# PEER gate spreading beside the u matmuls: second keys compared four tokens at once, routing weights applied on ScalarE

## The chip, the cores and the metric

The kernel runs on one core of one Trainium2 chip. The metric is the device time of one launch in microseconds. Names of engines in the trace: PE is TensorE (PEld its weight loads), DVE is VectorE, ACT is ScalarE, POOL is GpSimd, SP issues the DMAs.

## What is computed

Two trunk layers run over 288 tokens (256 prompt, 32 sample). Each layer has a token mixer and then a PEER block with 128 x 128 single-neuron experts. Only the PEER block matters here:

```python
def one_block(xb):
    q = (xb @ wq).reshape(blk, PEER_HEADS, 2, KEY_DIM)
    s = jnp.einsum('thcd,hcnd->thcn', q.astype(jnp.float32), keys.astype(jnp.float32))
    sv, si = lax.top_k(s, PEER_TOPK)
    ...
    expert = i1 * N_KEYS + i2
    gate = jax.nn.softmax(best, axis=-1)
    h = jnp.einsum('thkd,td->thk', u_tab[expert], xb)
    coef = (gate * jax.nn.gelu(h.astype(jnp.float32))).astype(xb.dtype)
    return jnp.einsum('thk,thkd->td', coef, v_tab[expert])
```

8 heads choose 16 experts each, so a token has 128 chosen experts, each with a first key, a second key and a softmax weight.

## The kernel before

**The PEER block computes every expert densely.** 128 weight tiles of `u` (32 groups `U` of RING = 4 tiles) each give one 128 x 288 block of `gelu(h)` in `acts`; it is multiplied by a dense gate matrix, which is zero but for the chosen experts, and then by 128 tiles of `v`. fp32 weights are split into a high and a low part and a product takes three matmuls (L608 to L610). For each half of a weight tile ScalarE copies the high part (`w_high`), GpSimd subtracts the low part (`w_low`), and the matmuls of a later tile use both. ScalarE makes the high part two tiles ahead, into the buffer that the half just multiplied leaves free, so its copy waits for that half's products.

**The gate matrix** is made for four tokens at a time, a batch: 72 batches a layer. For each token `one1` (128 slots x 128, one where the column is the slot's first key) and `one2` (the weight of the slot where the column is its second key) are multiplied on TensorE (`gates_of`, L779) into a PSUM bank, `bank[4]` for even batches and `bank[5]` for odd ones. `routed` transposed to `selT` holds first key, second key and weight of slot (partition) and token (column). `hot_iota` and `hot_tiles` are copies of the comparison rows in PSUM.

**The spreading stage** is where the change lies. It stands once in each layer beside 12 tiles of `u` (DURING), six batches a tile, three after each half. TensorE's order in a tile is: products of half a, batches 0, 1, 2, products of half b, batches 3, 4, 5. Even and odd here are also even and odd batches, since a tile begins at a multiple of six.

- VectorE: `onehots_of(k)` makes `one2` with four instructions of 128 columns (comparison and weight in one, L1478) and for even batches `one1` in one instruction of 512 (L1474). `weigh(k)` (L1485) multiplies the rows already in `acts` by the gate bank. It runs `weigh(k)` as soon as batch k is spread, and then `onehots_of(k + 2)`.
- ScalarE: in each half it first copies the high part (L1042), which waits for the products of that half; in half b the gelu of the tile follows (L1045). Then come three `keep_spread(k)` (L1032), which copies the rest of the gate bank once `weigh(k)` is done, and so lets TensorE overwrite the bank with batch k + 2.
- GpSimd: in a tile it subtracts the low part of half a (L589), makes `one1` of the odd batch 3 (`odd_onehot`, four instructions, L576), subtracts half b, makes `one1` of batch 5 and of batch 1 of the next tile. The `one1` of an odd batch waits for the odd batch before it.
- TensorE: batch k waits for `onehots`, for `odd_onehots` if odd, and for `spread_kept` of batch k - 2.

All engines run their own program in order; only semaphores tie them.

Of the kernel before, what the change touches and what calls it, by code (L numbers as in the profile page):

```python
# [33 lines left out]
ALU = mybir.AluOpType  # L34
ACT = mybir.ActivationFunctionType
AX = mybir.AxisListType

P = 128
# [62 lines left out]
def group(name, g):  # L101

    return g + FIRST[name]


def number(name, g, s):

    return RING * group(name, g) + s
# [7 lines left out]
BATCHES = T // 4  # L116
GGROUPS = 3
UREST = UGATED + GGROUPS
BEFORE, DURING = RING * UGATED, RING * GGROUPS
AFTER = BEFORE + DURING  # L120
TILE_BATCHES = BATCHES // DURING
HALF_BATCHES = TILE_BATCHES // 2

# [39 lines left out]
def build(nc, w_first, x_in, params_in, final_in, pool_first, ext_in, h0_in, w_in, w_pool, w_lru, w_ab, w_c, w_d, w_out,  # L163
          w_q, w_keys, w_u, w_v, x_keep, y_out, ext_out, h_out):
    with ExitStack() as ctx:
        def sem(name):
            return ctx.enter_context(nc.semaphore(name))
# [42 lines left out]
        selT = keep("selT", [3, T])  # L210
        o_one = cursor[0]
        one1 = [keep(f"one1_{b}", [4, P]) for b in range(2)]
        one2 = [keep(f"one2_{b}", [4, P]) for b in range(2)]
# [17 lines left out]
        def over(name, slot, c, dt=F32, skip=0):  # L231
# [77 lines left out]
            sem(n) for n in ("turned", "turned_out", "onehots", "spread", "spread_out"))  # L309
        odd_onehots, spread_kept, during_gated, tile_gated = (  # L310
            sem(n) for n in ("odd_onehots", "spread_kept", "during_gated", "tile_gated"))
        next_high, next_low = sem("next_high"), sem("next_low")
        stored, v_step, route_step = sem("stored"), sem("v_step"), sem("route_step")
        first_sem, last_sem = landed[0], route_step
# [139 lines left out]
        with nc.Fori(0, DEPTH) as layer:  # L454
            with nc.Block() as block:
# [146 lines left out]
                def _(pe):  # L602
# [60 lines left out]
                    for s, src in enumerate(("p_b", "xconv", "xconv", "xconv")):  # L663
                        pe.wait_ge(pooled if s == 0 else c_conv, 1)
                        high, low = pair[src]
                        for k0, wh, wl, count in halves("S", 0, s):
                            k0 += 4 * (s == 3)
                            for k in range(4):
                                if n >= 4:
                                    pe.wait_ge(extra_out, n - 3)  # L670
                                last = product(res[4 + n % 4], wh[:, k, :], wl[:, k, :],
                                               (high[:, k0 + k, :], low[:, k0 + k, :]), True, True)
# [29 lines left out]
                    for s in range(RING):  # L702
                        if s == LN_TILES[0]:
                            pe.wait_ge(d_conv, 1)
                            for k in range(CA):
                                last = nc.tensor.matmul(res[4], ones[:, :], cd[:, k, :], start=(k == 0), stop=(k == CA - 1))
                            last.then_inc(ln_sum1, 1)
                        tile("DG", 0, s, res[s], "x", evac=False)
                    for s in range(RING):
                        if s == LN_TILES[1]:  # L710
                            pe.wait_ge(ln_squared, 1)
                            for k in range(CA):
                                last = nc.tensor.matmul(res[4], ones[:, :], d_gate[:, k, :], start=(k == 0), stop=(k == CA - 1))
# [28 lines left out]
                    for s in range(RING):  # L742
                        for _, wh, wl, count in halves("KEYS", 0, s):
                            for tt in range(TILES):
                                if n >= 4:
                                    pe.wait_ge(scores_out, n - 3)
                                for c in range(4):
# [3 lines left out]
                                    last = product(out, qh, ql, (wh[:, c, :], wl[:, c, :]), True, True)  # L751
# [10 lines left out]
                    for j in range(3):  # L762
                        for tt in range(TILES):
                            r = TILE_ROWS[tt]
                            last = nc.tensor.transpose(bank[4 + j][:, tt * P:tt * P + r], routed[0:r, tt, j, :],
                                                       ident[0:r, 0:r])
                    last.then_inc(turned, 1)

                    def gates_of(k):

                        b = k % 2
                        pe.wait_ge(onehots, k + 1)
                        if b:
                            pe.wait_ge(odd_onehots, (k + 1) // 2)

                        if k > 1:
                            pe.wait_ge(spread_kept, k - 1)
                        for t in range(4):
                            last = nc.tensor.matmul(bank[4 + b][:, t * P:(t + 1) * P], one1[b][:, t, :],  # L779
                                                    one2[b][:, t, :], start=True, stop=True)  # L780
                        last.then_inc(spread, 1)

                    pe.wait_ge(turned_out, 1)
                    for m in range(DURING):
                        g, s = UGATED + m // RING, m % RING
                        pe.wait_ge(evacuated, RING * g + (EVAC["U"] + s - RING + 1))
                        for k0, wh, wl, n in halves("U", g, s):
                            for k in range(4):
                                last = product(res[s], wh[:, k, :], wl[:, k, :], (xh[:, k0 + k, :], xl[:, k0 + k, :]),
                                               k0 + k == 0, k0 + k == KC - 1)  # L790
# [64 lines left out]
                def _(act):  # L855
                    A = nc.scalar.activation
# [49 lines left out]
                    for s in range(RING):  # L906
                        for half in range(WIDTH["S"][s] // 4):
                            for k in range(4):
# [5 lines left out]
                                c = 4 * half + k + 4 * (s == 3)  # L914
# [20 lines left out]
                    for s in range(RING):  # L935
# [3 lines left out]
                        if s > 0:  # L939
                            last = tanh_of(2 * s - 2)  # L940
                    last = tanh_of(CC - 2)
# [55 lines left out]
                    for g in range(2):  # L997
                        for s in range(RING):
                            ahead("OUT", g, s)
                            c = 4 * g + s  # L1000
# [28 lines left out]
                    def keep_spread(k):  # L1029

                        act.wait_ge(spread_out, k + 1)
                        A(acts[:, AFTER:NKEYS + DURING, 4 * k:4 * k + 4],  # L1032
                          bank[4 + k % 2][:, :].rearrange("p (t i) -> p i t", t=4)[:, BEFORE:P, :], ACT.Copy)\
                            .then_inc(spread_kept, 1)

                    for m in range(DURING):
                        g, s = UGATED + m // RING, m % RING
                        grp, s2 = group("U", UGATED) + (m + 2) // RING, (m + 2) % RING
                        act.wait_ge(landed[s2], 16 * grp + 16)
                        for half in range(2):  # L1040
                            act.wait_ge(half_done, 2 * number("U", g, s) + half + 1)
                            A(w_high[2 * (s % 2) + half][:, :, :], raw[s2][:, 4 * half:4 * half + 4, :], ACT.Copy)\  # L1042
                                .then_inc(high_done, 1)
                            if half == 1:
                                A(acts[:, BEFORE + m, :], bank[s][:, 0:T], ACT.Gelu_apprx_tanh).then_inc(evacuated, 1)  # L1045
                            for b in range(HALF_BATCHES):
                                keep_spread(TILE_BATCHES * m + HALF_BATCHES * half + b)


                    act.wait_ge(spread, BATCHES)  # L1050
# [35 lines left out]

                    act.wait_ge(tile_gated, NKEYS - AFTER)
                    with act.Fori(0, GROUPS["VB"] - 1) as g:
# [31 lines left out]
                def _(dve):  # L1120
                    V = nc.vector
# [230 lines left out]
                    for g in range(2):  # L1352
                        for s in range(RING):
                            dve.wait_ge(half_done, 2 * number("OUT", g, s) + 2)
                            c = 4 * g + s
# [10 lines left out]
                    with dve.Fori(0, 4) as g:  # L1366
                        for s in range(RING):
                            dve.wait_ge(q_high_out, RING * g + (s + 1))
                            c = 4 * g + s
# [90 lines left out]
                    for j in range(3):  # L1460
                        last = V.tensor_copy(selT[:, j, :], bank[4 + j][:, 0:T])
# [3 lines left out]
                    hot_iota, hot_tiles = bank[7][:, 0:P], bank[7][:, P:2 * P]  # L1465
# [4 lines left out]
                    def onehots_of(k):  # L1470

                        b = k % 2
                        if b == 0:
                            V.tensor_tensor(one1[0][:, :, :], hot_iota.unsqueeze(1).to_broadcast([P, 4, P]),  # L1474
                                            selT[:, 0, 4 * k:4 * k + 4].unsqueeze(2).to_broadcast([P, 4, P]), ALU.is_equal)
                        for t in range(4):
                            c = 4 * k + t
                            last = V.tensor_scalar(one2[b][:, t, :], hot_tiles, selT[:, 1, c:c + 1], selT[:, 2, c:c + 1],  # L1478
                                                   ALU.is_equal, ALU.mult)
                        last.then_inc(onehots, 1)  # L1480

                    def weigh(k):

                        a = acts[:, 0:BEFORE, 4 * k:4 * k + 4]
                        V.tensor_tensor(a, a, bank[4 + k % 2][:, :].rearrange("p (t i) -> p i t", t=4)[:, 0:BEFORE, :],  # L1485
                                        ALU.mult).then_inc(spread_out, 1)
# [3 lines left out]
                    onehots_of(1)  # L1490
                    for k in range(BATCHES):
                        dve.wait_ge(spread, k + 1)
                        weigh(k)
                        if k + 2 < BATCHES:
                            onehots_of(k + 2)

                    dve.wait_ge(spread_kept, BATCHES)
                    for n in range(GGROUPS):
# [174 lines left out]
```

## Time and profile before

| | us |
|---|---|
| median of 3 runs | 3039.2 |
| lowest, highest | 3033.11, 3041.23 |
| time of the profiled execution | 3041.36 |
| its span | 3039.2 |

| engine | busy us | share |
|---|---|---|
| TensorE matmul | 2704.8 | 89% |
| GpSimd | 2237.4 | 74% |
| VectorE | 1926.3 | 63% |
| ScalarE | 1380.6 | 45% |

The span is the time from the first to the last instruction that the profiler saw. The shares are means over many stages with different limits, so they say little on one stage. The spreading stage of the first layer lies at about 799 to 965 us, that of the second at about 2304 to 2475 us. In a timeline row stand start, duration (of all instructions of the row together), engine, line, operation, output and inputs with shapes, the count, and in brackets the idle time ahead of the row with the instruction that ended it.

### The profile page before, as it was taken

To read this page: it belongs to the slowest core of one execution; us is meant where nothing else is said; L and a number is where in the kernel's file an instruction comes from. 1 tells how busy PE (TensorE), PEld (TensorE's weight loads), DVE (VectorE), ACT (ScalarE), POOL (GpSimd) and SP (SyncE) were. 2 spreads that over 40 slices of the span, in tenths; PEclk is the share of its full clock that TensorE was granted. 3 is DMA by queue.
4 is the path that set the end of the run, shared out by engine and by line. 5 is a ranking of instruction groups with operands and counts; after the bars stand their busy time and mean duration, and the time that the engine had idled before them with its cause. 6 is when DMAs were issued, how large, how long until landed. Compare 5 with 4: busy or idle time off the path is not lost. (4 is left out here: it accounts for less than half of the span.)

```text
span 3039.2 us, 60028 instructions
## 1 busy us (share of the span) xinstructions
PE 2704.8 (89%) x19546; PEld 2649.1 (87%) x19546; DVE 1926.3 (63%) x3651; ACT 1380.6 (45%) x2673; POOL 2237.4 (74%) x1819
## 2 busy tenths in 40 slices
PE   7778889999878999999987777899998789999997
PEld 6778879999867999999887777799997689999997
DVE  5699952797487345333676998429966863443336
ACT  4543344444423455555645433444443234455555
POOL 5676656799766878888766765568987678788886
PEclk9888989999999999999999999999999999999999
DMA  4334544445311555555443345444552125555554
GB/s 159 116 113 129 138 118 151 145 146 159 110 42 58 164 156 165 180 166 165 140 141 116 110 131 136 127 138 146 159 158 84 42 78 165 153 166 181 166 165 130
DMA packets 126240, 411.02 MB, mean 135 GB/s; under 512 B 20016, under 2 KB 24496, under 8 KB 125360
## 3 DMA queue, kind: packets, MB, share of 16 engines
q1 hardware_dynamic: 120160, 403.38, 43.3%
q10 hardware_dynamic: 5968, 6.22, 1.0%
q8 instruction: 62, 1.02, 0.1%
q14 instruction: 50, 0.41, 0.0%
HBM read 403.32 MB, written 6.22 MB: 135 GB/s over the span
## 5 line engine op out<-in xcount | busy, mean ns | idle before, releaser
L542 POOL TENSOR_TENSOR w_low<-raw,w_high 128x512 fp32r<-128x512 f32 x1450 | 1991.3, 1382 | 660.0 <-ACT w_high L863 584.0
L863 ACT ACTIVATE w_high<-raw 128x512 fp32r<-128x512 f32 x1266 | 796.7, 633 | 1166.0 <-PE bank L610 1158.6
L608 PE MATMUL bank<-xn_high,w_high 128*128 128x288 f32 x3456 | 1045.9, 303 | 74.8 <-POOL w_low L542 44.6
L609 PE MATMUL bank<-xn_low,w_high 128*128 128x288 f32 x3456 | 1031.8, 299 | 0.0
L610 PE MATMUL bank<-xn_high,w_low 128*128 128x288 f32 x3456 | 1027.6, 297 | 0.0
L608 PEld LDWEIGHTS bank<-xn_high,w_high 128*128 128x128 f32 x3456 | 661.2, 191 | 86.2 <-POOL w_low L542 53.9
L1512 DVE TENSOR_TENSOR c_lo<-acts,c_hi 128x288 fp32r<-128x288 f32 x352 | 380.9, 1096 | 448.0 <-ACT c_hi L1063 448.0
L610 PEld LDWEIGHTS bank<-xn_high,w_low 128*128 128x128 f32 x3456 | 662.1, 192 | 0.0
L609 PEld LDWEIGHTS bank<-xn_low,w_high 128*128 128x128 f32 x3456 | 661.7, 191 | 0.4
L608 PE MATMUL bank<-c_hi,w_high 128*128 128x288 f32 x2048 | 609.0, 297 | 10.0 <-DVE c_lo L1512 9.9
L610 PE MATMUL bank<-c_hi,w_low 128*128 128x288 f32 x2048 | 605.7, 296 | 0.0
L609 PE MATMUL bank<-c_lo,w_high 128*128 128x288 f32 x2048 | 605.2, 295 | 0.0
L608 PEld LDWEIGHTS bank<-c_hi,w_high 128*128 128x128 f32 x2048 | 386.1, 189 | 17.6 <-DVE c_lo L1512 9.7
L609 PEld LDWEIGHTS bank<-c_lo,w_high 128*128 128x128 f32 x2048 | 386.2, 189 | 0.1
L610 PEld LDWEIGHTS bank<-c_hi,w_low 128*128 128x128 f32 x2048 | 386.0, 188 | 0.0
L779 PE MATMUL bank<-one,one 128*128 128x128 f32 x1152 | 167.7, 292 | 91.5 <-issue 50.7
L779 PEld LDWEIGHTS bank<-one,one 128*128 128x128 f32 x1152 | 147.7, 200 | 107.7 <-issue 57.7
L1142 DVE SCALAR_TENSOR_TENSOR cd<-ext_d,par,cd 128x256 f32<-128x256 f32 x240 | 195.1, 813 | 7.8 <-DVE acc L1287 6.0
L576 POOL TENSOR_SCALAR one<-iota,selT 128x128 f32<-128x128 f32 x288 | 168.0, 601 | 41.0 <-PE bank L779 38.1
L1506 DVE TENSOR_TENSOR acts<-acts,ungated 128x288 f32 x80 | 97.7, 1222 | 154.6 <-ACT ungated L877 154.6
L1478 DVE TENSOR_SCALAR one<-bank,selT 128x128 f32<-128x128 f32 x576 | 195.3, 400 | 0.0
L1072 ACT ACTIVATE w_high<-raw 128x512 fp32r<-128x512 f32 x184 | 115.8, 629 | 114.0 <-PE bank L610 114.0
(232 smaller groups left out, 2776.3 us busy)
## 6 DMA issues: line engine op xcount, KB each, us to landing
raw<-w_u SPq DMA_DIRECT2D x256, 512.0 KB, 3.5
raw<-w_v SPq DMA_DIRECT2D x256, 512.0 KB, 3.5
raw<-w_in_t SPq DMA_DIRECT2D x136, 512.0 KB, 3.5
raw<-w_q SPq DMA_DIRECT2D x32, 512.0 KB, 3.5
raw<-w_ab SPq DMA_DIRECT2D x32, 256.0 KB, 2.7
raw<-w_c SPq DMA_DIRECT2D x16, 512.0 KB, 3.6
raw<-w_out_t SPq DMA_DIRECT2D x16, 512.0 KB, 3.6
raw<-w_first SPq DMA_DIRECT2D x12, 512.0 KB, 3.6
```

What stands on the lines that cost most here:

```text
L542: nc.gpsimd.tensor_tensor(w_low[slot][:, :, :], raw[s][:, 4 * half:4 * half + 4, :], w_high[slot][:, :, :].bitcast(F32), ALU.subtract)\
L576: last = nc.gpsimd.tensor_scalar(one1[1][:, t, :], iota[:, :], selT[:, 0, 4 * k + t:4 * k + t + 1], None, ALU.is_equal)
L608: nc.tensor.matmul(out, high, m_high, start=start, stop=False)
L609: nc.tensor.matmul(out, high, m_low, start=False, stop=False)
L610: return nc.tensor.matmul(out, low, m_high, start=False, stop=stop)
L779: last = nc.tensor.matmul(bank[4 + b][:, t * P:(t + 1) * P], one1[b][:, t, :], one2[b][:, t, :], start=True, stop=True)
L863: A(w_high[2 * (s % 2) + half][:, :, :], raw[s][:, 4 * half:4 * half + 4, :], ACT.Copy)\
L1072: A(w_high[2 * (s % 2) + half][:, :, :], raw[s2][:, 4 * half:4 * half + 4, :], ACT.Copy)\
L1142: did(V.scalar_tensor_tensor(o_p, pr, w, o_p, ALU.mult, ALU.add))
L1478: last = V.tensor_scalar(one2[b][:, t, :], hot_tiles, selT[:, 1, c:c + 1], selT[:, 2, c:c + 1], ALU.is_equal, ALU.mult)
L1506: V.tensor_tensor(acts[:, 4 * g + s, :], acts[:, 4 * g + s, :], ungated[s], ALU.mult)\
L1512: V.tensor_tensor(c_low[:, slot, :], acts[:, i, :], c_high[:, slot, :].bitcast(F32), ALU.subtract)\
```

## The change

Two tokens of an odd batch and all four of an even one (`HOT_FUSED` gives the first token that is treated so) get their `one2` in two steps: VectorE compares them in one instruction without the weight and signals `hot_seconds`; ScalarE multiplies each token's 128 columns by the weight, in place, and signals `hot_weighted`, for which TensorE waits as well. The comparison of the second keys is now the first thing in `onehots_of`. ScalarE's multiplication for batch k + 2 stands ahead of its `keep_spread(k)`. On VectorE `onehots_of(k + 2)` now stands ahead of `weigh(k)`.

```diff
+HOT_FUSED = (0, 2)
...
                         pe.wait_ge(onehots, k + 1)
+                        pe.wait_ge(hot_weighted, k + 1)
...
+                    def weigh_hot(k):
+
+                        act.wait_ge(hot_seconds, k + 1)
+                        for t in range(HOT_FUSED[k % 2], 4):
+                            c = 4 * k + t
+                            last = A(one2[k % 2][:, t, :], one2[k % 2][:, t, :], ACT.Identity, scale=selT[:, 2, c:c + 1])
+                        last.then_inc(hot_weighted, 1)
+
+                    weigh_hot(0)
+                    weigh_hot(1)
...
                             for b in range(HALF_BATCHES):
-                                keep_spread(TILE_BATCHES * m + HALF_BATCHES * half + b)
+                                k = TILE_BATCHES * m + HALF_BATCHES * half + b
+                                if k + 2 < BATCHES:
+                                    weigh_hot(k + 2)
+                                keep_spread(k)
...
                         b = k % 2
+                        f = HOT_FUSED[b]
+                        last = V.tensor_tensor(one2[b][:, f:, :], hot_tiles.unsqueeze(1).to_broadcast([P, 4 - f, P]),
+                                               selT[:, 1, 4 * k + f:4 * k + 4].unsqueeze(2).to_broadcast([P, 4 - f, P]),
+                                               ALU.is_equal)
+                        last.then_inc(hot_seconds, 1)
...
-                        for t in range(4):
+                        for t in range(f):
...
                         dve.wait_ge(spread, k + 1)
-                        weigh(k)
                         if k + 2 < BATCHES:
                             onehots_of(k + 2)
+                        weigh(k)
```

VectorE in the steady part of the stage, before. An even and an odd batch follow one another; `one_0` and `one_1` are the one-hot buffers, `acts<-acts,bank` is `weigh`:

```order
L1485 TENSOR_TENSOR acts<-acts,bank 128x76x4 [waits spread]
L1474 TENSOR_TENSOR one_0_75<-bank,selT 128x512
L1478 TENSOR_SCALAR one_0_77<-bank,selT 128x128 x4
L1485 TENSOR_TENSOR acts<-acts,bank 128x76x4 [waits spread]
L1478 TENSOR_SCALAR one_1_78<-bank,selT 128x128 x4
```

VectorE at the same place, after:

```order
L1490 TENSOR_TENSOR one_0_77<-bank,selT 128x512 [waits spread]
L1495 TENSOR_TENSOR one_0_75<-bank,selT 128x512
L1507 TENSOR_TENSOR acts<-acts,bank 128x76x4
L1490 TENSOR_TENSOR one_1_78<-bank,selT 128x256 [waits spread]
L1500 TENSOR_SCALAR one_1_78<-bank,selT 128x128 x2
L1507 TENSOR_TENSOR acts<-acts,bank 128x76x4
```

The comparison moved to the front, and `weigh` moved from the front of a batch to its end.

ScalarE from one high-part copy to the one of the other half, before (`acts<-bank 128x52x4` is `keep_spread`):

```order
L1042 ACTIVATE w_high_57<-raw_54 128x512 [waits half_done,landed3]
L1032 ACTIVATE acts<-bank 128x52x4 [waits spread_out] x3
L1042 ACTIVATE w_high_58<-raw_54 128x512 [waits half_done]
L1045 ACTIVATE acts<-bank 128x288
```

The same stretch of ScalarE, after:

```order
L1055 ACTIVATE w_high_57<-raw_54 128x512 [waits half_done,landed3]
L1044 ACTIVATE one_0_77<-one_0_77,selT 128x128 [waits hot_seconds]
L1044 ACTIVATE one_0_77<-one_0_77,selT 128x128 x3
L1035 ACTIVATE acts<-bank 128x52x4 [waits spread_out]
L1044 ACTIVATE one_1_78<-one_1_78,selT 128x128 [waits hot_seconds]
L1044 ACTIVATE one_1_78<-one_1_78,selT 128x128
L1035 ACTIVATE acts<-bank 128x52x4 [waits spread_out]
L1044 ACTIVATE one_0_77<-one_0_77,selT 128x128 [waits hot_seconds]
L1044 ACTIVATE one_0_77<-one_0_77,selT 128x128 x3
L1035 ACTIVATE acts<-bank 128x52x4 [waits spread_out]
L1055 ACTIVATE w_high_58<-raw_54 128x512 [waits half_done]
L1058 ACTIVATE acts<-bank 128x288
```

Ten multiplications, in three pieces that each wait for a comparison of VectorE, now stand between the two high-part copies, and the last `keep_spread` ahead of the second copy stands behind four of them.

## Rows read from the trace of the kernel before

**Rows 1.** Stretches: width, busy PE, PEld, DVE, ACT, POOL, clock, DMA share, GB/s.
```profile
760.00:800.00 40.00, 39.37 (x294) 38.67 (x292) 2.79 (x5) 22.15 (x41) 32.38 (x25) 1.00 0.55 169
860.00:900.00 40.00, 28.79 (x209) 27.03 (x210) 34.71 (x98) 10.52 (x26) 27.50 (x42) 0.96 0.14 41
```

**Rows 2.** Waits, 803 to 962 us: us in total, times, longest us.
```profile
PE bank L779 <- issue: 23.2, 11, 2.1
PE bank L779 <- DVE one L1478: 19.7, 25, 1.5
```

**Rows 3.** Timeline of TensorE, one tile; L608 x1 is a half's first product.
```profile
855.11 1.13 PE L779 MATMUL bank<-one,one 128*128 128x128 f32 x8 [2.11 <-issue]
855.99 0.38 PE L608 MATMUL bank<-xn_high,w_high 128*128 128x288 f32 x1
...
857.67 2.23 PE L779 MATMUL bank<-one,one 128*128 128x128 f32 x16
861.16 1.16 PE L779 MATMUL bank<-one,one 128*128 128x128 f32 x8 [1.26 <-DVE one L1478]
862.08 0.38 PE L608 MATMUL bank<-xn_high,w_high 128*128 128x288 f32 x1
...
865.07 1.16 PE L779 MATMUL bank<-one,one 128*128 128x128 f32 x8 [0.27 <-DVE one L1478]
868.34 1.13 PE L779 MATMUL bank<-one,one 128*128 128x128 f32 x8 [2.11 <-issue]
869.23 0.38 PE L608 MATMUL bank<-xn_high,w_high 128*128 128x288 f32 x1
```

**Rows 4.** Timeline of VectorE, same tile.
```profile
856.27 0.47 DVE L1485 TENSOR_TENSOR acts<-acts,bank 128x304 f32<-128x304 f32 x1 [0.58 <-PE bank L779]
...
858.76 0.47 DVE L1485 TENSOR_TENSOR acts<-acts,bank 128x304 f32<-128x304 f32 x1 [0.74 <-PE bank L779]
859.15 0.68 DVE L1474 TENSOR_TENSOR one<-bank,selT 128x512 f32<-128x512 f32 x1
859.75 1.36 DVE L1478 TENSOR_SCALAR one<-bank,selT 128x128 f32<-128x128 f32 x4
861.03 0.46 DVE L1485 TENSOR_TENSOR acts<-acts,bank 128x304 f32<-128x304 f32 x1
```

**Rows 5.** Timeline of ScalarE, same tile.
```profile
861.52 0.34 ACT L1032 ACTIVATE acts<-bank 128x208 f32<-128x208 f32 x1 [1.91 <-DVE acts L1485]
...
863.95 0.63 ACT L1042 ACTIVATE w_high<-raw 128x512 fp32r<-128x512 f32 x1 [0.43 <-PE bank L610]
864.49 0.39 ACT L1045 ACTIVATE acts<-bank 128x288 f32<-128x288 f32 x1
```

**Rows 6.** Timeline of GpSimd, same tile.
```profile
864.66 1.27 POOL L589 TENSOR_TENSOR w_low<-raw,w_high 128x512 fp32r<-128x512 f32 x1 [2.33 <-ACT w_high L1042]
865.91 2.33 POOL L576 TENSOR_SCALAR one<-iota,selT 128x128 f32<-128x128 f32 x4
```

**Rows 7.** Instruction groups of ScalarE, shapes kept apart: busy us, mean ns.
```profile
L932 ACT ACTIVATE rg<-rg,lru 128x288 f32<-128x288 f32 x16 | 7.4, 526 | 0.0
...
L888 ACT ACTIVATE ext_c<-bank 128x256 f32<-128x256 f32 x16 | 5.9, 367 | 0.0
...
L916 ACT ACTIVATE y_b<-bank,par 128x288 f32<-128x288 f32 x8 | 3.3, 503 | 0.0
...
L889 ACT ACTIVATE ext_c<-bank 128x32 f32<-128x32 f32 x16 | 3.1, 194 | 0.0
...
L982 ACT ACTIVATE d_gate<-cd 128x1152 f32<-128x1152 f32 x2 | 2.3, 1157 | 0.0
```

**Rows 8.** Timeline of ScalarE: activations with a per-partition scale, back to back.
```profile
96.33 0.39 ACT L877 ACTIVATE yg<-bank 128x288 f32<-128x288 f32 x1
96.62 1.66 ACT L916 ACTIVATE y_b<-bank,par 128x288 f32<-128x288 f32 x4
...
130.79 0.95 ACT L932 ACTIVATE rg<-rg,lru 128x288 f32<-128x288 f32 x2
```

More of the change, by code:

```diff
@@ L311, in build @@
             sem(n) for n in ("odd_onehots", "spread_kept", "during_gated", "tile_gated"))
+        hot_seconds, hot_weighted = sem("hot_seconds"), sem("hot_weighted")
         next_high, next_low = sem("next_high"), sem("next_low")
@@ L1472, in onehots_of @@
                         b = k % 2
+                        f = HOT_FUSED[b]
[3 more added lines that the diff above has]
+                        last.then_inc(hot_seconds, 1)
                         if b == 0:
-                            V.tensor_tensor(one1[0][:, :, :], hot_iota.unsqueeze(1).to_broadcast([P, 4, P]),
-                                            selT[:, 0, 4 * k:4 * k + 4].unsqueeze(2).to_broadcast([P, 4, P]), ALU.is_equal)
-                        for t in range(4):
+                            last = V.tensor_tensor(one1[0][:, :, :], hot_iota.unsqueeze(1).to_broadcast([P, 4, P]),
+                                                   selT[:, 0, 4 * k:4 * k + 4].unsqueeze(2).to_broadcast([P, 4, P]),
+                                                   ALU.is_equal)
+                        for t in range(f):
                             c = 4 * k + t
```

## The prediction, made before the changed kernel ran

> **What bounds the kernel now.** The page was read first for the whole (TensorE 89% busy), and then the busy time by stretch [rows 1]. Ahead of the stage that the change touches TensorE is busy 39.37 of 40 us, inside it only 28.79 of 40. The stage is where TensorE waits, and only there can the change act. The granted clock was 0.96 of full speed inside, against 1.00 ahead of it, so the clock explains little of the gap.
>
> The list of waits tells for whom TensorE waits in the stage [rows 2]: 25 waits on VectorE's `one2` (19.7 us) and 11 of about 2.1 us that end in "issue" (23.2 us), a wait whose releaser the profile didn't find. The timelines give it a name. The tile is strictly periodic: its first product starts at 855.99 and the next tile's at 869.23, so a tile takes 13.24 us [rows 3]. TensorE idles three times in it: 1.26 before batch 2 and 0.27 before batch 4, both for `one2`, and 2.11 before batch 5. Batch 5 starts at 868.34, and GpSimd's `one1` ends at 865.91 + 2.33 = 868.24 [rows 6]. So the "issue" wait is for GpSimd. It is the wait that ends last in the tile, and it isn't touched by the edit.
>
> What sets GpSimd's time is a loop through all four compute engines. Start to start, beginning at batch 0 [rows 3 to 6]:
> - batch 0 at 857.67, VectorE's `weigh` at 858.76: 1.09
> - `weigh`, then `one1`: 0.39; `one1`, then the four `one2`: 0.60; these to batch 2 at 861.16: 1.41
> - batch 2 to the products of half b at 862.08: 0.92
> - these to ScalarE's high-part copy at 863.95: 1.87
> - copy to GpSimd's subtraction at 864.66: 0.71; to its four comparisons at 865.91: 1.25; to batch 5 at 868.34: 2.43
> - batch 5 to the next tile's products: 0.89; a half's products (855.99 to 857.67): 1.68
>
> The sum is 13.24, the whole period. Any change of a member moves all 24 tiles (12 in each layer). Whatever lies outside, such as batches 1, 3 and 4, is free as long as it stays outside. The VectorE wait of 1.26 is inside the loop, the one of 0.27 is not: batch 4 could come earlier, and batch 5 would still wait for GpSimd.
>
> **The prices.** (1) Comparison of four tokens in one instruction: the `one1` instruction has the same form, 0.68 long and 0.60 to the next one [rows 4]. The one of two tokens in an odd batch replaces two of 0.32 each ((861.03 - 859.75) / 4) and is no longer than half of 0.60 and a start, so odd batches get no later on VectorE. (2) The multiplication on ScalarE, 128 columns in SBUF with a per-partition scale, is not in the trace. The nearest are 288 columns of the same form, 0.526 long; two in a row took 0.95, so the second began 0.95 - 0.526 = 0.42 behind the first [rows 7, 8]. The slope is 0.77 ns a column from 32 to 256 columns ((367 - 194) / 224) and 0.88 from there to 1152 ((1157 - 367) / 896) [rows 7]; 160 columns fewer at the middle, 0.83, are 0.13. So the multiplication lasts 0.526 - 0.13 = 0.39, and when several follow each other one costs 0.42 - 0.13 = **0.29**. The lower bound is 0.22, from the form that reads PSUM: four in 1.66, (1.66 - 0.50) / 3 = 0.39 apart [rows 7, 8], less 0.17, which is 160 columns at 1.07 ns, the step from a copy of 288 columns (0.29 to the next start) to one of 512 (0.54) [rows 5, 8]. The upper bound is 0.39, if they don't overlap when they work in place. I take 0.29, since its row reads and writes SBUF as the new one does. (3) `keep_spread` is 0.34 long [rows 5]; the instruction behind it starts 0.09 before its end, as the gelu starts 0.54 behind a copy of 0.63 [rows 5], so it holds the queue for 0.25. (4) Handovers: VectorE to ScalarE 0.03 to 0.04 (861.49 to 861.52), others 0.05 to 0.10. (5) Identity needs no table load: `y_b`, an Identity, follows a gelu directly [rows 8]. (6) TensorE waits for one more semaphore in each batch; where it isn't late I cost it at nothing, since TensorE's 16 gate matmuls of two batches run through without a gap over such waits [rows 3]; at most some 0.03 for each of six batches in a tile.
>
> **The loop after the change**, with batch 0 started at 0:
> - VectorE starts the comparison for batch 2 at 1.09; ScalarE can start at 1.09 + 0.68 + 0.04 = 1.81
> - four multiplications: 1.81 + 4 x 0.29 = 2.97. Then `keep_spread` of batch 0, whose `weigh` is now behind both comparisons on VectorE and ends at 1.09 + 0.60 + 0.60 + 0.46 = 2.75, just in time. It ends at 2.97 + 0.34 = 3.31, and batch 2 starts at **3.36**. Before, it started at 3.49: the shorter comparison gained 0.13 and no more, since ScalarE and then the copy of the bank are in line behind it.
> - the products of half b are done as before 0.92 + 1.87 = 2.79 later, at 6.15, and ScalarE could copy the high part. But ScalarE's queue is in order, and ahead of that copy now stand four multiplications for batch 4, which wait for a comparison that waits for batch 2. Batch 2 is seen by VectorE 1.16 after its start (855.11 to 856.27) [rows 3, 4]: 4.52. Comparison: 4.52 + 0.72 = 5.24. Multiplications: 6.40. `weigh` of batch 2 ends at 4.52 + 1.66 = 6.18. `keep_spread`: 6.65.
> - the high-part copy starts at **6.65**, against 3.49 + 2.79 = 6.28 before: 0.37 later. From here nothing changes: 0.71 + 1.25 + 2.43 + 0.89 + 1.68 = 6.96.
>
> The period is 13.61, 0.37 more than 13.24. Over 24 tiles that is **+8.9 us**. The VectorE wait of TensorE goes, and its place is taken by ScalarE's queue, which delays GpSimd. What is behind the waiting multiplications on ScalarE is thus the term that decides. The start of a stage has a few tenths on either side (batch 0 no longer waits for eight instructions, but the first high-part copy waits for six multiplications), which I leave at zero. VectorE itself gets free: for two batches 0.60 + 0.60 + 0.38 and 0.33 + 0.64 + 0.38 = 2.93 us instead of 3.9, so its busy share in the stage falls by a quarter, and this costs or gives nothing.
>
> The profiled execution took 3041.4 us over a span of 3039.2; plus 8.9 it would be 3050.3. It was 2.2 above the median of the runs (3039.2), so against the median the forecast is **3048 us**.
>
> **What the Trainium skill says.** VectorE applies the weight within the comparison, at 0.32 us for 128 columns with both steps [rows 4]. The Trainium skill, page "ScalarE: Activation LUTs", section "Rules for kernel authors", says that multiplications belong on VectorE and not on ScalarE; that speaks against this change, and the trace agrees as far as the sum above goes, since a comparison of 0.72 and four multiplications (1.16) take 1.88 in line where 1.36 stood. The same page, section "What ACT_TABLE_LOAD costs", gives 186 ns + 0.833 ns a column, 93 ns for a per-partition operand and 93 ns of overlap; by it a multiplication would cost an estimated 0.29 us, and the sum would come out the same +9 us.
>
> **Rivals.**
> - *Hidden.* If a multiplication costs 0.22, batch 2 is bound by `weigh` (2.75) and starts at 3.17, the multiplications for batch 4 end at 5.93 and `weigh` at 5.99, and the high-part copy starts at 6.27, as before. The period stays 13.24, the time 3039 (3035 to 3043). For it speaks the PSUM form's price, against it that both operands are in SBUF. With multiplications that cost less still it gets no better, as `weigh` was moved behind the comparisons on VectorE.
> - *ScalarE becomes the bound for good* (slower). If the multiplications don't overlap, four take 1.57: batch 2 starts at 1.81 + 1.57 + 0.34 + 0.05 = 3.77, the copy at 3.77 + 1.16 + 0.72 + 1.57 + 0.25 = 7.47, 1.19 later than before. 24 tiles give +28.5, or 3068. It decides from 0.29 up: each 0.01 more on a multiplication costs 0.08 a tile, 1.9 us in all. The two-in-0.95 row speaks against it, small delays of the waits between ScalarE's instructions for it.
> - *The waits for VectorE go and nothing takes their place* (faster). Then 1.26 + 0.27 a tile are gained, 36.7 us: 3002. It would need GpSimd's `one1` to come as much earlier. Against it: GpSimd is held by the copy of half b, which is held by batch 2. It could be so in part if ScalarE's queue ran shorter than I have it, or if GpSimd's instructions got shorter with VectorE less busy; their 2.33 to 2.34 doesn't vary within the stage.
>
> **Chances.** My forecast, a small loss of 4 to 15 us: 0.50. Hidden, within 4 us: 0.18. ScalarE bound, 15 to 35 us lost: 0.20. Faster by more than 9 us: 0.12. About 0.3% (9.1 us) is what a measurement of this kernel can tell from no change. The forecast lies right at that edge, so its 0.50 splits, 0.27 within and 0.23 beyond: same 0.45, slower 0.43, faster 0.12. The range that leaves out 2 in 10 reaches from just below the hidden case to the bound of multiplications that don't overlap: 3034 to 3068.
>
> **What would show it.** In the trace after: the tile's period in the stage (13.6); ScalarE's multiplications 0.29 apart; TensorE's waits for VectorE gone, smaller ones before batch 2 for ScalarE (about 1.1, batch 2 starting 3.36 behind batch 0), and the "issue" wait before batch 5 grown from 2.11 to about 2.9 (it takes over the 0.27 of batch 4, the 0.13 that batch 2 is earlier, and the 0.37); GpSimd waiting longer for the high part of half b, its own durations unchanged. I am wrong if the high-part copy of half b doesn't start later behind batch 0 than 6.28, or if batch 5 no longer ends GpSimd's loop.

## The result, and the profile after

The changed kernel took 3073.8 us (median of 4 runs, 3072.0 to 3075.4) against 3036.2 us for the kernel before beside it: a ratio of 1.0124, 95% interval 1.0108 to 1.0141, or +37.6 us. The forecast was 3048 us, its range ended at 3068, and so the time lies outside. The sign of the forecast sum was right, its size (8.9 us) was a quarter of what came.

The page of the changed kernel, engines' busy time and the granted clock in 40 slices:

```profile
span 3071.4 us, 60244 instructions
...
PE 2714.0 (88%) x19546; PEld 2662.8 (87%) x19546; DVE 1862.9 (61%) x3363; ACT 1506.4 (49%) x3105; POOL 2239.6 (73%) x1819
...
PEclk9899989999988999999988989999999899999999
```

VectorE has 63 us less to do and ScalarE 126 us more, as the edit says. The new group on ScalarE in the first layer's stage (out, in, shape, count, busy us, mean ns, idle ahead):

```profile
L1044 ACT ACTIVATE one<-one,selT 128x128 f32<-128x128 f32 x212 | 69.5, 390 | 57.4 <-DVE one L1490 57.4
```

Each multiplication is 0.390 us long, as estimated (0.39). In the second layer two tiles ran with the granted clock at 1.00 throughout; such tiles are called undisturbed here. One of them on TensorE, which answers to [rows 3] (L610 x1 is a half's first product, L782 a batch):

```profile
2334.51 2.11 PE L782 MATMUL bank<-one,one 128*128 128x128 f32 x16
2339.79 1.13 PE L782 MATMUL bank<-one,one 128*128 128x128 f32 x8 [3.16 <-POOL one L578]
2340.67 0.38 PE L610 MATMUL bank<-xn_high,w_high 128*128 128x288 f32 x1
...
2342.36 1.05 PE L782 MATMUL bank<-one,one 128*128 128x128 f32 x8
2343.61 1.13 PE L782 MATMUL bank<-one,one 128*128 128x128 f32 x8 [0.20 <-POOL one L578]
2345.82 1.13 PE L782 MATMUL bank<-one,one 128*128 128x128 f32 x8 [1.08 <-ACT acts L1035]
2346.71 0.38 PE L610 MATMUL bank<-xn_high,w_high 128*128 128x288 f32 x1
```

And ScalarE and GpSimd in it, which answer to [rows 5] and [rows 6]:

```profile
2344.17 1.28 ACT L1044 ACTIVATE one<-one,selT 128x128 f32<-128x128 f32 x4 [0.88 <-DVE one L1490]
2345.36 0.32 ACT L1035 ACTIVATE acts<-bank 128x208 f32<-128x208 f32 x1
...
2347.72 1.28 ACT L1044 ACTIVATE one<-one,selT 128x128 f32<-128x128 f32 x4 [0.87 <-DVE one L1490]
2348.90 0.32 ACT L1035 ACTIVATE acts<-bank 128x208 f32<-128x208 f32 x1
2349.12 0.62 ACT L1055 ACTIVATE w_high<-raw 128x512 fp32r<-128x512 f32 x1
```

```profile
2335.96 1.27 POOL L591 TENSOR_TENSOR w_low<-raw,w_high 128x512 fp32r<-128x512 f32 x1 [2.93 <-ACT w_high L1055]
2337.20 2.33 POOL L578 TENSOR_SCALAR one<-iota,selT 128x128 f32<-128x128 f32 x4
```

The loop is the forecast one. Batch 0 starts at 2342.36, batch 2 3.46 later (forecast 3.36), ScalarE's high-part copy at 2349.12, which is 6.76 later (6.65), directly behind four multiplications and the gate copy. The idle before batch 5 is 3.16 us, not 2.11. From one copy (2335.26) to the next (2349.12) the tile takes 13.86 us; 13.61 was forecast and 13.24 was the tile before.

But most tiles are longer. Two successive tiles in the first layer, TensorE:

```profile
845.09 1.13 PE L782 MATMUL bank<-one,one 128*128 128x128 f32 x8 [3.15 <-POOL one L578]
845.97 0.38 PE L610 MATMUL bank<-xn_high,w_high 128*128 128x288 f32 x1
...
846.60 0.45 PE L611 MATMUL bank<-xn_low,w_high 128*128 128x288 f32 x1
...
848.52 2.64 PE L782 MATMUL bank<-one,one 128*128 128x128 f32 x16
...
855.25 2.10 PE L782 MATMUL bank<-one,one 128*128 128x128 f32 x16
860.51 2.05 PE L782 MATMUL bank<-one,one 128*128 128x128 f32 x8 [3.16 <-POOL one L578]
862.21 0.59 PE L610 MATMUL bank<-xn_high,w_high 128*128 128x288 f32 x1
...
864.52 1.95 PE L782 MATMUL bank<-one,one 128*128 128x128 f32 x16
867.99 1.13 PE L782 MATMUL bank<-one,one 128*128 128x128 f32 x8 [1.52 <-ACT acts L1035]
```

In the second of them (from 855.25) batch 5 lasts 2.05 us and not 1.13 behind the same idle of 3.16 us, and the next half's products take 862.21 to 864.52 = 2.31 us and not 1.69. The granted clock of three stretches of it (width, busy TensorE, clock, DMA share, GB/s):

```profile
857.30:860.50 3.20, 0.05 (x1) 0.95 0.36 101
860.50:863.90 3.40, 3.39 (x16) 0.54 0.15 59
863.90:867.00 3.10, 2.57 (x22) 1.00 0.00 0
```

0.50 is 1.2 GHz, 1.00 is 2.4 GHz. TensorE stood idle for 3.2 us, began its work at the lower level and kept it over batch 5 and the first six of the twelve products behind it (the seventh starts at 863.73). In the tile ahead the fall came later: batch 5 (845.09) still ran at full clock behind 3.15 us of idle, and only from 1.5 us after its start, with the fifth product (846.60), was the clock at 0.50. The products took 845.97 to 848.52 = 2.55 us, and the two batches behind them 2.64 us and not 2.11. The two forms alternate: the clock fell in 22 of the 24 tiles, in 11 of them just ahead of batch 5 and in 11 among the products behind it.

All 11 tile lengths of the first layer are 15.3 to 15.4 us; in the second two are 13.86 and nine 15.3 to 15.4. The kernel before had the same thing in 9 of its 24 tiles. Its tile at 836 to 851 us:

```profile
840.43 2.05 PE L779 MATMUL bank<-one,one 128*128 128x128 f32 x8 [2.12 <-issue]
```

```profile
841.00:842.00 1.00, 1.00 (x6) 0.50 0.12 45
```

That tile took 14.68 us (from half b's products to the next half b's, as all lengths here); 7 of the 22 tile lengths before are 14.5 to 16.1, the others 13.22 to 13.25. In both layers they begin at every third tile; why there, no run shows. The Trainium skill, page "TensorE: Matmul & The Clock Gate", section "What's actually happening", says that TensorE's clock falls to half when it is idle and is given back by activity; the trace agrees in both levels.

The lengths of the 22 tiles make the sum. Above their undisturbed length (13.24 and 13.87) they have 11.1 us in the kernel before and 29.8 us in the changed one: the clock costs 18.7 us more. Each kernel has one more fall behind the last tile length of each layer (963.61 and 2472.09 before, 983.40 and 2505.74 after), which is in neither sum. The loop costs 24 x 0.63 = 15.1 us. Together 33.8 us, where the two spans differ by 32.2.

### The profile page after: what moved, and what is told of

The parts are those of the page before. It is cut to its first block and busy times, and to the rows that moved or that the text cites. A ratio compares the mean times of both kernels' runs of the same rounds, so it can differ in the third digit from the quotient of the medians.

```text
span 3071.4 us, 60244 instructions
## 1 busy us (share of the span) xinstructions
PE 2714.0 (88%) x19546; PEld 2662.8 (87%) x19546; DVE 1862.9 (61%) x3363; ACT 1506.4 (49%) x3105; POOL 2239.6 (73%) x1819
## 5 line engine op out<-in xcount | busy, mean ns | idle before, releaser
L610 PE MATMUL bank<-xn_high,w_high 128*128 128x288 f32 x3456 | 1048.9, 303 | 76.0 <-POOL w_low L544 45.1
L610 PEld LDWEIGHTS bank<-xn_high,w_high 128*128 128x128 f32 x3456 | 663.6, 192 | 87.8 <-POOL w_low L544 55.0
L610 PE MATMUL bank<-c_hi,w_high 128*128 128x288 f32 x2048 | 608.1, 297 | 10.0 <-DVE c_lo L1534 9.9
L610 PEld LDWEIGHTS bank<-c_hi,w_high 128*128 128x128 f32 x2048 | 385.2, 188 | 17.5 <-DVE c_lo L1534 9.8
L782 PE MATMUL bank<-one,one 128*128 128x128 f32 x1152 | 170.0, 300 | 113.1 <-POOL one L578 76.3
L782 PEld LDWEIGHTS bank<-one,one 128*128 128x128 f32 x1152 | 156.5, 212 | 123.8 <-issue 119.6
L1044 ACT ACTIVATE one<-one,selT 128x128 f32<-128x128 f32 x432 | 141.5, 391 | 119.0 <-DVE one L1490 119.0
```

What stands on the lines that cost most here:

```text
L610: nc.tensor.matmul(out, high, m_high, start=start, stop=False)
L1044: last = A(one2[k % 2][:, t, :], one2[k % 2][:, t, :], ACT.Identity, scale=selT[:, 2, c:c + 1])
```

## The experiments

The theory so far: (a) ScalarE's multiplications stand in its queue ahead of the high-part copy, and that lengthens the loop that GpSimd closes; (b) the longer idle that results before batch 5 lets TensorE's clock fall in nearly every tile. Rivals: all of it is queues, or ScalarE's work itself is the cost. All ratios are against the kernel before, run on the same chip beside the variant. Where two variants weren't run side by side and differ by a few us, the tile lengths decide, not the times.

**Extra work in the idle gap, changed kernel.** This tests the clock alone. TensorE gets matmuls on constants into an unused bank ahead of the wait for batch 5; the result isn't touched.

```diff
                         b = k % 2
+                        if k % TILE_BATCHES == 5:
+                            for _ in range(10):
+                                nc.tensor.matmul(bank[6][:, 0:P], ident[:, :], iota[:, :], start=True, stop=True)
```

> The changed kernel with ten more fp32 matmuls of 128x128x128 on constants into an unused PSUM bank, on TensorE ahead of its wait for batch 5 of each tile, where it idles 3.16 us. Clock theory: of the 37 us that the change lost, about 15 are a longer loop (tile of 13.86 us where the granted clock stays at 1.00) and about 20 are half clock behind the 3.16 us of idle, in nearly each tile (15.3 to 15.4 us each). With TensorE busy the clock stays up, each tile takes about 13.9 us, and the time is about 3073.8 - 30 = 3044 us. Rival theory, that the longer tiles come from the queues alone: the extra matmuls change nothing or add a little, 3074 to 3080 us.

Measured 3038.7 us, ratio 1.000 (0.999 to 1.0009). A tile of TensorE (L776 are the extra matmuls, each of which stands as two in the count), GpSimd's `one1` ahead of that batch 5, and the stage (columns as in [rows 1]):

```profile
852.33 2.40 PE L776 MATMUL bank<-iota,ident 128*128 128x128 f32 x20
855.67 1.13 PE L785 MATMUL bank<-one,one 128*128 128x128 f32 x8 [0.94 <-POOL one L578]
```

```profile
853.07 2.34 POOL L578 TENSOR_SCALAR one<-iota,selT 128x128 f32<-128x128 f32 x4
```

```profile
803.00:962.00 159.00, 133.16 (x1050) 126.69 (x1050) 105.17 (x241) 100.01 (x310) 108.13 (x159) 1.00 0.12 37
```

Batch 5 still starts 0.26 us after GpSimd is done (855.41), but at full clock, and every one of the 22 tile lengths is 13.86 to 13.89 us. More work on the busiest engine took 35 us off; the tile lengths account for 30 of them. That is (b), shown.

**The same, kernel before**, with six extra matmuls.

> The kernel before with six such matmuls ahead of the wait for batch 5, where it idles 2.11 us. Clock theory: the 7 or 8 tiles of 14.5 to 16.1 us among the 24 fall to 13.24 us, about 11 us less: 3025 us. Rival theory (queues alone set the period): no change, 3036 us.

Measured 3025.2 us, ratio 0.9953 (0.9936 to 0.9970), all tile lengths 13.23 to 13.26. The kernel before had itself been paying for its clock: 11.1 us by the 22 tile lengths, some 14 by the ratio (9 to 19). Between the two kernels with extra work, both at full clock, lie 13.5 us: this is the loop's share alone (24 x 0.63 = 15).

**The copy moved ahead of the multiplications**, changed kernel. In ScalarE's program the high-part copy of half b, with its gelu, comes before the last batch of half a:

```diff
                             for b in range(HALF_BATCHES):
+                                if half == 0 and b == HALF_BATCHES - 1:
+                                    copy_high(1)
                                 k = TILE_BATCHES * m + HALF_BATCHES * half + b
```

> The changed kernel with one thing moved: ScalarE copies the high part of half b (and makes the tile's gelu) ahead of the multiplications for batch 4 and the gate copy of batch 2, not behind them. Queue theory: the copy starts 6.15 us behind batch 0 and not 6.75, so GpSimd's loop is 0.6 us a tile shorter; batch 4 gets later but batch 5 still waits longest. Period about 13.3 us at full clock; the idle before batch 5 falls from 3.16 to about 1.1 us with 1.4 us before batch 4, so the clock falls seldom: 3030 to 3040 us. Rival (ScalarE's multiplications themselves are the cost wherever they stand): the loss of the loop stays, at least 3045 us.

Measured 3057.6 us, ratio 1.0060 (1.0043 to 1.0078). The profiled run was the fastest of four with 3047.1; the other three took 3057.5 to 3059.5 at a lower mean clock (0.954 to 0.957 against 0.960), so its trace shows fewer falls than they had. The mechanism came, the time didn't. Undisturbed tiles are 13.34 us, 0.53 less than 13.87 and 0.10 above the kernel before, so the loss of the loop came from the place in ScalarE's queue and not from its work: (a), shown. TensorE in a tile of it:

```profile
864.61 1.13 PE L782 MATMUL bank<-one,one 128*128 128x128 f32 x8 [1.61 <-ACT acts L1035]
866.69 2.04 PE L782 MATMUL bank<-one,one 128*128 128x128 f32 x8 [0.96 <-POOL one L578]
```

The 3.16 us of idle became 1.61 and 0.96, with one batch between, and the clock fell all the same: 8 of the 22 lengths are 14.6 to 16.2 us, and each fall begins close to the start of batch 5. I had expected that shorter gaps would keep it up. That they failed to because they stand close together is my reading and isn't tested by itself; what speaks for it is the version with GpSimd out of the loop, below, where idles of 1.2 and 1.5 us stand half a tile apart and the clock never fell.

**Each part alone**, both with ten extra matmuls, so that the clock is nearly out of it. First only VectorE's order, in the kernel before:

```diff
                         dve.wait_ge(spread, k + 1)
-                        weigh(k)
                         if k + 2 < BATCHES:
                             onehots_of(k + 2)
+                        weigh(k)
```

> The kernel before with only the order on VectorE changed (the one-hot comparisons of batch k + 2 ahead of the gate multiplication of batch k), and with ten extra matmuls on constants ahead of batch 5, so that the clock stays up; it is to be compared with the kernel before under extra matmuls (3025 us, 13.25 us a tile). Loop theory: the gate bank is copied only after 0.60 + 1.28 us of comparisons more, so batch 2 starts 3.85 us behind batch 0 (3.49 before), and the high-part copy, now behind the gate copy of batch 2, starts 7.63 behind it (6.28): period about 14.6 us, 3025 + 33 = 3058 us. Rival (the order alone is harmless, since VectorE does the same work): 3025 us.

Then only the split, the changed kernel with VectorE's old order:

```diff
                         dve.wait_ge(spread, k + 1)
+                        weigh(k)
                         if k + 2 < BATCHES:
                             onehots_of(k + 2)
-                        weigh(k)
```

> The changed kernel with VectorE's old order (gate multiplication first), with ten extra matmuls ahead of batch 5. Loop theory: the comparison starts 0.39 us later, and ScalarE's four multiplications with it, so batch 2 starts 3.75 us behind batch 0 and the high-part copy 7.43: period about 14.5 us, 3056 us, against 3039 us for the changed kernel under extra matmuls. So the two parts of the change would each be worse alone than together. Rival (the cost is in the multiplications' number alone, which is the same here): 3039 us.

Measured 3063.6 us (1.0086, 1.0069 to 1.0103) and 3061.4 us (1.0081, 1.0064 to 1.0097); undisturbed tiles of 14.69 and 14.63 us against 14.6 and 14.5 expected. The clock fell in four and in five tiles all the same (up to 15.4 us), about 3 us in each run. Against 3025 and 3039 us both parts alone are worse than both together. Each lengthens the way from batch 0 to the gate copy by itself, the order by putting comparisons ahead of `weigh`, the split by putting ScalarE's multiplications in line. Together they overlap: `weigh` runs on VectorE while ScalarE multiplies (2348.20 to 2348.66 and 2347.72 to 2349.00 in the changed kernel).

**Fewer waits on TensorE**, changed kernel with ten extra matmuls.

```diff
-                        pe.wait_ge(onehots, k + 1)
-                        pe.wait_ge(hot_weighted, k + 1)
+                        if k < 2:
+                            pe.wait_ge(onehots, k + 1)
+                            pe.wait_ge(hot_weighted, k + 1)
```

The gate copy that TensorE waits for anyway comes behind both on their engines.

> The changed kernel with ten extra matmuls ahead of batch 5, in which TensorE waits from batch 2 of a stage on only for the gate copy (spread_kept) and GpSimd's one1; ScalarE's gate copy of batch k - 2 follows its multiplications for batch k and VectorE's comparisons for batch k, so the two waits left out say nothing more. Theory: TensorE starts a late batch 0.10 to 0.16 us later than before for each of the two late batches of a tile because of the longer list of waits (0.26 us behind GpSimd's end, not 0.10). Without them the period falls from 13.87 to about 13.6 us: 3039 - 6 = 3033 us. Rival (the delay has another cause): 3039 us.

Measured 3034.6 us, ratio 0.9991 (0.9982 to 1.0001), against 3038.7 and 1.000 with all waits. The two intervals meet, so the times alone don't show a gain; the tiles do, 13.62 to 13.65 us against 13.86 to 13.89. GpSimd and TensorE in a tile of it:

```profile
851.02 2.33 POOL L578 TENSOR_SCALAR one<-iota,selT 128x128 f32<-128x128 f32 x4
```

```profile
853.41 1.16 PE L786 MATMUL bank<-one,one 128*128 128x128 f32 x8 [0.80 <-POOL one L578]
```

GpSimd ends at 853.35 and batch 5 starts 0.06 later; with all waits it was 0.26, in the changed kernel (2339.53 to 2339.79) as with the ten matmuls. Batch 2 starts 0.06 behind the end of the gate copy (845.68 to 845.74), where it was 0.14 (2345.68 to 2345.82). The tile is now 13.63, and 13.61 was the prediction's sum. So the 0.25 us that the sum lacked are the two late starts of TensorE behind its longer list of waits.

**GpSimd out of the loop**, changed kernel: VectorE makes the `one1` of odd batches too, in one 512-wide comparison. GpSimd's instructions for them and TensorE's wait for `odd_onehots` go with it.

```diff
-                        if b == 0:
-                            last = V.tensor_tensor(one1[0][:, :, :], hot_iota...
+                        if True:
+                            last = V.tensor_tensor(one1[b][:, :, :], hot_iota...
```

> The changed kernel with the one1 of odd batches made on VectorE in one 512-wide comparison, as the even ones are, and not on GpSimd. If GpSimd's comparisons close the loop, it opens: TensorE then waits for the gate copies only (about 1.2 us before batch 2 and 1.4 us before batch 5), period about 12.1 us, clock at 1.00, and the time is about 3036 - 26 - 11 = 3000 us. If the loop isn't closed by GpSimd, VectorE's added 1.8 us a tile make it slower than 3074 us.

Measured 2999.1 us, ratio 0.9864 (0.9847 to 0.9882), tiles of 12.23 to 12.25 us, none longer. TensorE's waits in the first layer's stage are now for ScalarE's gate copy, 1.2 us before batch 2 and 1.5 before batch 5:

```profile
PE bank L773 <- ACT acts L1026: 32.9, 24, 1.5
```

With GpSimd's comparisons gone the change's spare time on VectorE is worth something. Whether it is the change that makes the room, the kernel before with the same move tells:

```diff
-                        if b == 0:
-                            V.tensor_tensor(one1[0][:, :, :], hot_iota...
+                        if True:
+                            V.tensor_tensor(one1[b][:, :, :], hot_iota...
```

> The kernel before with the one1 of odd batches on VectorE and nothing of the change: no multiplications on ScalarE, old order. Question: is it the change that makes room for them on VectorE? Theory: VectorE has 2 x (0.38 + 0.60 + 1.28) = 4.52 us for two batches, so it is the bound at 13.56 us a tile, with four idle gaps of TensorE of about 1 us each; the clock stays up, and the time is 3025 + 0.3 x 24 = 3033 us, against 2999 us with the split. Rival (opening GpSimd's loop is all that counts, the split brings nothing): about 3000 us.

Measured 3030.9 us, ratio 0.9971 (0.9960 to 0.9983), tiles of 13.53 us, 2 of 22 of them 14.3. Its waits in the first layer's stage (us in total, times, longest), and the stage:

```profile
PE bank L770 <- DVE one L1469: 46.5, 47, 1.5
```

```profile
803.00:962.00 159.00, 113.23 (x841) 104.27 (x839) 158.32 (x423) 39.78 (x105) 29.82 (x24) 0.99 0.11 37
```

VectorE, busy 158.3 of 159 us, is the bound there, as worked out, and the change (the split and the order together) takes 32 us off that kernel. With the change and the shorter list of waits as well:

```diff
-                        pe.wait_ge(onehots, k + 1)
-                        pe.wait_ge(hot_weighted, k + 1)
+                        if k < 2:
+                            pe.wait_ge(onehots, k + 1)
+                            pe.wait_ge(hot_weighted, k + 1)
```

> The version with one1 of odd batches on VectorE (2999 us, 12.24 us a tile), in which TensorE waits from batch 2 on only for the gate copy. Theory: here too a late start is 0.1 us shorter without the two waits, at batches 2 and 5: period about 12.05 us, 2999 - 4 = 2995 us. Rival: 2999 us.

Measured 2997.1 us, ratio 0.9856 (0.9838 to 0.9874), tiles of 12.11 us instead of 12.24: 0.13 x 24 = 3 us. The intervals of the two overlap, the tile lengths don't.

**A faster version.** All `one1` on VectorE, `HOT_FUSED = (2, 2)`, VectorE's old order, and ScalarE's high-part copy of half b moved forward as above.

```diff
-HOT_FUSED = (0, 2)
+HOT_FUSED = (2, 2)
...
-                        if b == 0:
+                        if True:
...
                         dve.wait_ge(spread, k + 1)
+                        weigh(k)
                         if k + 2 < BATCHES:
                             onehots_of(k + 2)
-                        weigh(k)
```

> A version meant to be faster: all one1 on VectorE; two tokens of each batch, even or odd, by the fused comparison and ScalarE, two by VectorE alone; VectorE's old order (gate multiplication first); ScalarE's high-part copy of half b ahead of the multiplications for batch 4. Theory: two multiplications and not four on ScalarE's piece for even batches, so the gate copy comes sooner; TensorE's waits are short and spread over the tile; period about 11.8 to 12.0 us against 12.24 in the version with one1 on VectorE alone: 2999 - 8 = 2991 us. If ScalarE's queue isn't what binds there, 2999 us or more.

Measured 2990.1 us, ratio 0.9846 (0.9829 to 0.9862). It beats the kernel before by about 47 us. All tiles are 11.82 to 11.84 us. What each of the three steps beyond `one1` on VectorE gave wasn't measured. TensorE's idle gaps in it and the stage:

```profile
851.07 1.16 PE L773 MATMUL bank<-one,one 128*128 128x128 f32 x8 [0.39 <-DVE one L1496]
853.02 1.16 PE L773 MATMUL bank<-one,one 128*128 128x128 f32 x8 [0.79 <-DVE one L1496]
...
857.70 2.33 PE L773 MATMUL bank<-one,one 128*128 128x128 f32 x16 [1.03 <-ACT acts L1026]
```

```profile
803.00:950.00 147.00, 119.88 (x903) 111.08 (x902) 145.21 (x359) 84.46 (x255) 35.14 (x27) 1.00 0.14 44
```

VectorE is busy 145 of 147 us, the clock never falls. VectorE is now the bound of the stage.

## Why the prediction was wrong, point by point

- **The bound** was read rightly: GpSimd's `one1` ended the longest wait ("issue"), and it closed a loop of four engines. With its comparisons on VectorE the tile fell from 13.9 to 12.2 us.
- **The prices** were right: 0.39 us for a multiplication (measured 0.390); 0.29 from one to the next (four last 1.28, so they start 0.89 / 3 = 0.30 apart); 0.25 for a gate copy (2348.90 to 2349.12 = 0.22). One slip changes nothing: the step from 0.29 to 0.54 over 224 columns is 1.12 ns a column and not 1.07, which puts the lower bound at 0.21 and not 0.22. GpSimd's own durations didn't change (2.33, 1.27).
- **The loop after the change** was right in its mechanism and mis-sized by 0.25 us a tile, 13.86 against 13.61. The step that failed in it is (6), the further semaphore on TensorE, costed at nothing where it isn't late. Its bound of 0.03 a batch was read where TensorE was late itself. Where TensorE waits, the rest of the list comes behind the signal: 0.26 us instead of 0.10 at batch 5, and 0.14 instead of 0.05 at batch 2. Taking two waits out of the list gave 13.63. The loop's term is then 15.1 us, not 8.9.
- **The clock** is the step that was missing, and the larger part of the miss. The prediction said of 0.96 in the stage that "the clock explains little of the gap" and took the tile of 855.99 to 869.23 for strictly periodic. That tile was one of those in which the clock didn't fall. The row for 860 to 900 us [rows 1] with its 0.96 already held such a fall, and a tile further back in the same trace shows it (840.43, 2.05 us for a batch instead of 1.13). The text even listed that the idle before batch 5 would grow from 2.11 to 2.9 us (it grew to 3.16), and never asked what that does to the clock. The sum had no term for it. It cost 18.7 us: 29.8 in the changed kernel, 11.1 before.
- **The rivals.** "Hidden" needed a multiplication of 0.22 and got 0.30. "ScalarE becomes the bound", at +28.5 us, had the time nearest to the measured one, and that would have been luck: its mechanism is out, since the multiplications do overlap. "Nothing takes their place" is out.
- **The rule on multiplications.** The Trainium skill, page "ScalarE: Activation LUTs", section "Rules for kernel authors", puts them on VectorE, for its speed per element. Where GpSimd closed the loop, the change that moved them to ScalarE lost, as the rule would have it. With GpSimd out of the loop and VectorE the bound, the same change took 3030.9 to 2999.1 us.

The sum with both terms at their measured size: 3036.2 + 15.1 + 18.7 = 3070, against 3073.8 measured. The 4 us that are left lie within the spread of the kernel before (medians of 3036 to 3040 us in four groups of runs).

## What to carry to other kernels

When TensorE waits, look at the granted clock of single microseconds around the wait and at several periods, not at one clean one: a change that makes the gap longer can cost more through the half clock that follows than through the gap. Ahead of moving work to a less busy engine, write down what stands behind it in that engine's queue and which loop that belongs to; the share of busy time (45% here) says nothing on it. A freed engine brings time only once the thing that ends last is given to it.

## What the runs showed of the hardware

- With 3.16 us of idle in each tile TensorE's clock fell to 0.50 in 22 of 24 tiles: in 11 of them just ahead of the batch that ends the idle, which then took 2.05 us and not 1.13, and in 11 some 1.5 us after that batch had started, so that the batch itself shows nothing. With 2.11 us of idle it fell in 9 of 24 tiles. With 1.61 and 0.96 us and one batch between them 8 of 22 tile lengths were long; with 1.2 and 1.5 us half a tile apart none was. With the 3.16 us gap filled by matmuls that nobody needs the clock stayed at 1.00, and the kernel was 35 us faster.
- A wait of TensorE that is satisfied late delays the start by the waits that stand beside it: 0.26 us from GpSimd's end to batch 5 with four semaphores in the list, 0.10 with three, 0.06 with two; 0.14 us to batch 2 with three, 0.05 with two, 0.06 with one. So the number of waits isn't all of it; in what order they are taken wasn't tried.
- Activations of 128 columns with a per-partition scale, in place in SBUF, start 0.30 us apart and last 0.39.
